# Adding the first slot of each chunk on VectorE instead of TensorE, in a product-key expert layer

## The reference

```
q = (xt @ w_query).reshape(t, 8, 2, 128)
sk = einsum('thcd,ckd->thck', q, sub_keys)          # two sets of 128 keys
top_s, top_i = top_k(sk, 16)                        # product keys: 16 x 16 candidates
idx, gate = the 16 best of the candidates, softmax of their scores      # per token, per head
h = einsum('thkd,td->thk', peer_u[idx], xt)
a = gate * gelu(h)
out = einsum('thk,thkd->td', a, peer_v[idx])        # 8 heads x 16 experts = 128 rows of 1024 per token
x = x + out
```

## Time and profile before

| what | value |
|---|---|
| median of 3 runs | 3075.08 us (3071.18 to 3080.69) |
| profiled execution, first to last instruction (span) | 3067.0 us |
| what the metric has around the span | 8.1 us (3075.08 - 3067.0); the profiled execution has no other time than its span |
| PE, DVE busy | 2694.1 us (88%), 2135.5 us (70%) |
| ACT, POOL busy | 1193.2 us (39%), 1260.2 us (41%) |
| DMA | 1170.33 MB, mean 382 GB/s |
| chain that ended last | PE 43%, DMA 22%, DVE 20%, ACT 8%, issue 5%, POOL 2% |

### The profile page before, as it was taken

One profiled execution on the slowest core, in us unless ns is written; L12 is line 12 of the kernel. 1 busy time (PEld: TensorE's weight loads), 2 busy tenths in 40 slices (PEclk: granted clock), 3 DMA queues, 4 the chain that ended last, 5 costly groups with the idle time before them and its releaser, 6 DMA issues.

```text
span 3067.0 us, 29307 instructions
## 1 busy us (share of the span) xinstructions
PE 2694.1 (88%) x8608; PEld 1481.6 (48%) x8608; DVE 2135.5 (70%) x5243; ACT 1193.2 (39%) x3444; POOL 1260.2 (41%) x1028
## 2 busy tenths in 40 slices
PE   7869899989998999788998999888999877877777
PEld 6656465445654555345554555435555332333333
DVE  4555577976657778866656778876756777776765
ACT  3322445753324545533223545653323323232232
POOL 0023343344334454444444444334444555445443
PEclk9789999999999999899999999989999999889989
DMA  4269999999999999999999999989999999999998
GB/s 160 67 255 414 368 397 394 378 354 401 398 420 415 407 419 417 361 358 404 413 415 420 397 378 421 393 331 368 412 420 421 420 418 422 405 420 417 418 416 353
DMA packets 173808, 1170.33 MB, mean 382 GB/s; under 512 B 19280, under 2 KB 19408, under 8 KB 42576
## 3 DMA queue, kind: packets, MB, share of 16 engines
q0 software_dynamic: 147456, 1073.81, 86.0%
q1 hardware_dynamic: 26192, 94.65, 8.1%
HBM read 1166.28 MB, written 2.10 MB: 381 GB/s over the span
## 4 chain that ended last, share of the span: by engine, by line
PE 43%; DMA 22%; DVE 20%; ACT 8%; issue 5%; POOL 2%; SPq 0%; DVEq 0%; ACTq 0%
PE ysum L543 29%; DMA gather<-experts,idx 22%; DVE gather L1028 10%; PE bank L404 9%; DVE sd L811 3%; PE bank L505 3%; ACT diag L750 2%; POOL gather L362 2%; ACT amp L742 2%; ACT L592 1%; PE bank L451 1%; PE bank L419 1%; ACT gel L735 1%; DVE shared L838 1%; ACT sd L592 1%
## 5 line engine op out<-in xcount | busy, mean ns | idle before, releaser
L543 PE MATMUL ysum<-gather,diag 128*128 128x512 f32 x4096 | 1920.7, 624 | 300.1 <-ACT diag L750 298.6
L362 POOL DMA_INDIRECT gather<-experts,idx x1024 | 1260.0, 1230 | 1785.1 <-PE ysum L543 1519.9
L1028 DVE CUSTOM_DVE_ANT_0 gather<-gather,xc 128x1024 f32<-128x1024 f32 x1024 | 1222.8, 1224 | 545.3 <-DMA gather<-experts,idx 543.0
L543 PEld LDWEIGHTS ysum<-gather,diag 128*128 128x128 f32 x4096 | 802.5, 200 | 1320.2 <-issue 926.5
L735 ACT ACTIVATE gel<-hdot 128x4 f32<-128x4 f32 x255 | 52.4, 205 | 1519.2 <-DVE hdot L1028 1501.7
L404 PE MATMUL bank<-xnT,w 128*128 128x256 f32 x1984 | 457.2, 385 | 7.4 <-DVE xnT L800 7.4
L404 PEld LDWEIGHTS bank<-xnT,w 128*128 128x128 f32 x1984 | 376.6, 192 | 86.0 <-issue 29.9
L750 ACT ACTIVATE diag<-cc,amp 128x128 f32<-128x128 f32 x1020 | 326.8, 387 | 35.8 <-PE ysum L543 35.0
L742 ACT ACTIVATE amp<-gel,gate 128x1 f32<-128x1 f32 x1020 | 216.9, 283 | 8.3
L811 DVE RECIPROCAL sd<-sd 128x256 f32<-128x256 f32 x60 | 105.1, 1751 | 128.5 <-ACT sd L592 128.3
L735 ACT ACT_TABLE_LOAD x124 | 159.1, 1283 | 2.2
(11 more groups left out here) (116 smaller groups left out, 1495.2 us busy)
## 6 DMA issues: line engine op xcount, KB each, us to landing
w<-weights SPq DMA_DIRECT2D x168, 512.0 KB
gather<-experts,idx POOLq DMA_INDIRECT x1024
y_out<-x SPq DMA_DIRECT2D x4, 512.0 KB, 8.0
x<-x_in SPq DMA_DIRECT2D x2, 512.0 KB, 5.3
g2b<-g_rows SPq DMA_DIRECT2D x2, 512.0 KB
x<-x_in SPq DMA_DIRECT2D x1, 1024.0 KB, 12.0
cc<-consts_in SPq DMA_DIRECT2D x1, 603.5 KB, 6.6
late<-late_in SPq DMA_DIRECT2D x2, 256.0 KB, 9.9
```

Source lines behind the costliest of these rows:

```text
L362: pool.indirect_dma_start(gather[:, n % SLOTS, :], None, uv_d[m // 2], bass.IndirectOffsetOnAxis(ap=idx[:, g % 2, k:k + 1], axis=0)).then_ ...
L543: mm = nc.tensor.matmul(ysum[:, hf * 512:(hf + 1) * 512], diag[:, n % NDIAG, :], gather[:, n % SLOTS, DM + hf * 512:DM + (hf + 1) * 512], ...
L1028: e = V.tensor_tensor_reduce(out=gather[:, n % SLOTS, 0:DM], in0=gather[:, n % SLOTS, 0:DM], in1=xc[:, :], scale=1.0, scalar=0.0, op0=ALU. ...
```

## The change

Slot 0 of each chunk (`n % 4 == 0`) no longer goes to PE. DVE multiplies the second half of its row with `amp` and adds it to a new SBUF buffer `yacc` (`add_slot`); at the first chunk of a tile pass it writes instead of adding. It does so for chunk `cg - 1` behind the four dots of chunk `cg`. `s_yv` counts these, and POOL waits on it for a buffer whose last slot was such a slot; the other three slots wait on `s_yc` as before, whose counts are now three a chunk. ACT makes no diagonal for slot 0. `add_tile` adds both `ysum` and `yacc` to `x`. The DMA scratch area that the program reserves in SBUF is set to 4096 bytes a partition.

```diff
+        yacc = sb("yacc", DM)
+        s_yv = sem("s_yv")
+        def free(eng, n):
+            if n % CH == 0:
+                eng.wait_ge(s_yv, n // CH + 1)
+            else:
+                eng.wait_ge(s_yc, pe_slots(n) + 1)
+        def pe_slots(n):
+            return n // CH * (CH - 1) + n % CH - 1
...
                         if n >= SLOTS:
-                            pool.wait_ge(s_yc, n - SLOTS + 1)
+                            free(pool, n - SLOTS)
                         pool.indirect_dma_start(
...
         def chunk_pe(pe, c):
-            for j in range(CH):
+            for j in range(1, CH):
...
-                pe.wait_ge(s_dg, n + 1)
+                pe.wait_ge(s_dg, pe_slots(n) + 1)
                 for hf in range(2):
-                    mm = nc.tensor.matmul(ysum[:, hf * 512:(hf + 1) * 512], diag[:, n % NDIAG, :],
+                    mm = nc.tensor.matmul(ysum[:, hf * 512:(hf + 1) * 512], diag[:, pe_slots(n) % NDIAG, :],
                                           gather[:, n % SLOTS, DM + hf * 512:DM + (hf + 1) * 512],
-                                          start=k == 0, stop=k == HEADS * TOPK - 1)
+                                          start=k == 1, stop=k == HEADS * TOPK - 1)
...
         def diagonals(act, c):
...
-            for j in range(CH):
+            for j in range(1, CH):
...
             def add_tile(tg):
-                dve.wait_ge(s_yc, (tg + 1) * HEADS * TOPK)
+                dve.wait_ge(s_yc, (tg + 1) * (HEADS * TOPK // CH) * (CH - 1))
                 t = tg % (SEQ // P)
-                V.tensor_tensor(x[:, t, :], ysum[:, :], x[:, t, :], ALU.add).then_inc(s_x, 1)
+                chain(dve, V.tensor_tensor(x[:, t, :], ysum[:, :], x[:, t, :], ALU.add))
+                V.tensor_tensor(x[:, t, :], yacc[:, :], x[:, t, :], ALU.add).then_inc(s_x, 1)
+            def add_slot(cg):
+                n = cg * CH
+                dve.wait_ge(s_a, n + 1)
+                row = gather[:, n % SLOTS, DM:2 * DM]
+                scale = amp[:, cg % 2, 0:1]
+                if cg:
+                    dve.wait_ge(s_yv, cg)
+                if cg % per_tile == 0:
+                    V.tensor_scalar(yacc[:, :], row, scale, None, ALU.mult).then_inc(s_yv, 1)
+                else:
+                    V.scalar_tensor_tensor(yacc[:, :], row, scale, yacc[:, :], ALU.mult, ALU.add).then_inc(s_yv, 1)
...
+                if cg:
+                    add_slot(cg - 1)
                 if c % per_tile == 0 and cg:
+                    dve.wait_ge(s_yv, cg)
                     add_tile(cg // per_tile - 1)
...
             if m == NBLK - 1:
+                add_slot(NBLK * CHUNKS - 1)
+                dve.wait_ge(s_yv, NBLK * CHUNKS)
                 add_tile(m * TT + 1)
...
-    nc = bacc.Bacc("TRN2", target_bir_lowering=False, num_devices=1)
+    nc = bacc.Bacc("TRN2", target_bir_lowering=False, num_devices=1, dynamic_dma_scratch_size=4096)
```

More of the change, by code:

```diff
@@ L532, in chunk_pe @@
         def chunk_pe(pe, c):
-            for j in range(CH):
+            for j in range(1, CH):
                 n = c * CH + j
                 k = n % (HEADS * TOPK)
-                if k == 0 and n:
+                if k == 1 and n > 1:
                     pe.wait_ge(s_x, n // (HEADS * TOPK))
-                pe.wait_ge(s_dg, n + 1)
+                pe.wait_ge(s_dg, pe_slots(n) + 1)
                 for hf in range(2):
-                    mm = nc.tensor.matmul(ysum[:, hf * 512:(hf + 1) * 512], diag[:, n % NDIAG, :],
+                    mm = nc.tensor.matmul(ysum[:, hf * 512:(hf + 1) * 512], diag[:, pe_slots(n) % NDIAG, :],
                                           gather[:, n % SLOTS, DM + hf * 512:DM + (hf + 1) * 512],
-                                          start=k == 0, stop=k == HEADS * TOPK - 1)
+                                          start=k == 1, stop=k == HEADS * TOPK - 1)
                 mm.then_inc(s_yc, 1)
@@ L726, in last_diagonals @@
                                      scale=gate[:, c // 4 % 2, k:k + 1]).then_inc(s_a, 1)
-                act.wait_ge(s_a, n + 1)
-                act.wait_ge(s_yc, n - NDIAG + 1)
-                nc.scalar.activation(diag[:, n % NDIAG, :], ident, ACT.Copy, scale=amp[:, c % 2, j:j + 1]).then_inc(s_dg, 1)
+                if j:
+                    p = pe_slots(n)
+                    act.wait_ge(s_a, n + 1)
+                    act.wait_ge(s_yc, p - NDIAG + 1)
+                    nc.scalar.activation(diag[:, p % NDIAG, :], ident, ACT.Copy, scale=amp[:, c % 2, j:j + 1])\
+                        .then_inc(s_dg, 1)
         def diagonals(act, c):
@@ L743, in diagonals @@
                                      scale=gate[:, c // 4 % 2, k:k + 1]).then_inc(s_a, 1)
-            for j in range(CH):
+            for j in range(1, CH):
                 n = c * CH + j
+                p = pe_slots(n)
                 act.wait_ge(s_a, n + 1)
-                if n >= NDIAG:
-                    act.wait_ge(s_yc, n - NDIAG + 1)
-                nc.scalar.activation(diag[:, n % NDIAG, :], ident, ACT.Copy, scale=amp[:, c % 2, j:j + 1]).then_inc(s_dg, 1)
+                if p >= NDIAG:
+                    act.wait_ge(s_yc, p - NDIAG + 1)
+                nc.scalar.activation(diag[:, p % NDIAG, :], ident, ACT.Copy, scale=amp[:, c % 2, j:j + 1]).then_inc(s_dg, 1)
         def peer_act(act, m):
```

## The result

The changed kernel takes 3978.79 us (median of 4, 3974.83 to 3980.06) against 3074.67 us for the one before on the same chip: ratio 1.294, 95% interval 1.292 to 1.296. 4055 us was forecast (1.319), in a range of 3800 to 4290.

A forecast was written before the change was run, and what follows sets the result against it. DMA transfers were taken as the floor before; after, a queue emptying once a chunk. 253 periods of 14.41 us with start and end give 3889, plus 142 and 22: 4053 us span, 4061 with 8.1; 4055 us put, range 3800 to 4290.

The forecast's parts named there:

- Only one gather in flight at the release: When add_slot(c) frees buffer 4c, only gather 4c + 8 can be in flight, so the DMA queue empties once a chunk.
- PE was to be below 60% busy: Sign listed as showing the forecast right: PE's busy share, 88% before, falls below 60%.
- The cycle of 14.41 us: From one buffer release to the next: 0.28 + 11.55 + 1.15 + 1.28 + 0.15 us, against 11.1 us a chunk before.
- POOL held up by DVE, 0.15 us a chunk: POOL's issue takes 1.87 us when a dot starts just before it, 0.94 otherwise; 0.15 us a chunk taken, ends 0 and 0.93.
- The latency fit: Skill's fit for a gather, 2.0 us plus bytes over 436 GB/s: 4.4 us against 5.68, making the sum 330 us less.
- Weight loads and late DVE chunks, 164 us: 134 weight loads, 0.85 of them counted, 142 us; DVE's routing and mixer slices beyond the hidden 8.5 us, 22 us.
- The sum: 3889 us from the periods and the end, plus 142 and 22: 4053 us of span, 4061 with 8.1 us around it.
- The gain (2964 us): Faster rival: release early enough, queue never empties, DMA at its best rate throughout, 2964 us; chance 0.03.
- The smaller scratch: Rival: the smaller DMA scratch holds fewer gathers at once; if only one fitted, 6100 us; chance 0.03.
- The 8.1 us: Time around the profiled span, added to 4053 us to give 4061; said to be all that separates span and runs.
- the shorter gap: Rival, same mechanism: landings at 10.64 us, no POOL delay, period 13.35 us, about 3730 us; chance 0.13.
- the longer one: Rival, same mechanism: third dot at 12.08 us, full 0.93 us POOL delay, period 15.72 us, about 4410 us; chance 0.09.

The follow-up runs named there:

- the hold alone: Kernel before, plus only POOL waiting to reuse slot 4c's buffer until the four dots of chunk c + 1 are done: 3796.63 us, ratio 1.234.
- the kernel with small loads: Changed kernel with each of the 134 weight loads after the first 34 cut to an eighth of its bytes: 3889.04 us, ratio 1.267.
- Added work alone: Kernel before plus one DVE multiply-add behind each chunk's dots, on data no gather touches, and the 4096-byte scratch: 3106.41 us, ratio 1.011.
- Three in flight: Changed kernel with add_slot(c) placed ahead of the third dot of chunk c + 1, same work: 3302.41 us, ratio 1.077.

## Why the prediction was right

*Only one gather in flight at the release.* Right. POOL waits for the add in 246 chunks, the DMA share is near the forecast one (0.76 in the last block, "0.7 to 0.75" was said; 287 GB/s, 290 was said), the hold alone reproduces four fifths of the loss, one buffer more gives 61% of it back. One sign failed: PE was to be below 60% busy and is at 66%, since its matmuls took longer at the lower granted clock (last section), which costs nothing here.

*The cycle of 14.41 us.* 14.66 in the last block. Its terms there: 0.27 (0.28 said), third landing 11.97 (11.55 + 0.15 said), 1.15, 1.28. The period after an undisturbed POOL issue is 14.38 (44 of 60), where I had 14.26: 0.12 x 253 = 30 us more. The three landings come 5.90, 9.47 and 11.97 us after POOL's start on average in the last block, where the first gathers of the run gave 5.68, 9.06 and 11.55. Gather 565 was not the only other one of the kernel before that met an empty queue, as the prediction has it: from 2034 to 2036 us the DMA share is 0.00 too, ahead of gather 637, whose dot VectorE took late.

*POOL held up by DVE, 0.15 us a chunk.* Right as a mean: 39 of 253 first issues lasted 1.5 us or more, and their periods were longer by 1.05 us in the last block (16) and 0.71 us before it (23), 33 us in all against 38.

As the Trainium skill says (SBUF — State Buffer, "SBUF: two separate sides"), a GpSimd operation that reads SBUF and starts behind a VectorE operation with two SBUF inputs waits it out: the issue takes 1.91 us at 3719.06, behind a dot, and 0.94 at 3705.07, in the trace above. Issues behind `add_tile`'s second add (both inputs in SBUF) take 1.82 us, those behind its first add (one input in PSUM) 0.94 us, 7 of each.

The latency fit of the Trainium skill (DMA: Bandwidth & Descriptors, "Anatomy of one DMA — SWDGE (gpsimd) path") gives an estimate of 4.4 us for such a gather; here it is 5.9 us on average in the last block (5.21 us in the shortest of its periods), and the measurement decides.

*Weight loads and late DVE chunks, 164 us.* The term that was mis-sized. Undisturbed periods are 14.70 us in blocks 0 to 2 and 14.38 in block 3: 0.32 x 192 = 61 us for both causes. I had put 0.85 of the loads' bytes beside flowing gathers. By the kernel with small loads they cost some 15 us: the DMA rests about 3.6 us in each cycle (share 0.75 of 14.66 us).

*The sum.* Minus 103 for that, plus 30 for the landings, minus 5 for POOL, plus 5 since the first gather went out at 193.7 us instead of 188.9, minus 2.5 since the end is 9.9 us behind the last dot, not 12.4: 75 us less than 4053, 3978; the span is 3978.3. The 8.1 us that the prediction adds around the span is not what the metric has there: every execution on record is 1.8 us longer than its span (3980.06 against 3978.3 here), and the rest of the 8.1 was the difference between two executions. With 1.8 the sum of 4053 gives the 4055 that was put, by luck. The prediction's 11.1 us a chunk (2864 over 256) is 11.2; nothing hangs on it.

*Rivals.* The gain (2964 us) is excluded by the kernel with slot 0 in no sum: even without DVE's part it is 3050. The smaller scratch made no difference with nine gathers in flight (3070.12 us). Added work alone is 37 us. The undisturbed period of 14.38 us lies between the 13.35 of the shorter gap and the 15.72 of the longer one: from an empty queue the landings were not spaced evenly, and the full 0.93 us of a held-up issue fell in 39 periods alone.

## What to carry to other kernels

Where one queue of transfers sets the pace, ask of every consumer that is moved how long it holds its buffer, and count the transfers still in flight when it lets go; that count times the time of one transfer must at least cover the hand-over plus the latency of a transfer from an empty queue (here 2.7 + 5.7 us against 2.5 for the one gather in flight). Three in flight, 7.5 us, are short of it (11.04 us a chunk). And it is a least count: four, 10 us, would cover it, and the kernel with four (the add ahead of the 2nd dot) still took 10.56 us a chunk in the last block against 10.09. 1.28 us of work on an engine with 543 us to spare cost 904 us where it stood, and 37 us where no buffer waited for it. An engine at 88% that stands in the chain may be waited for only because all buffers are full: leave its work out in a test before moving it.

## What the hardware showed that I had not expected

PE did a quarter fewer of its largest matmuls and was busy for only 54 us less (2639.9 against 2694.1): one took 759 ns on average where it had 624:

```profile
L554 PE MATMUL ysum<-gather,diag 128*128 128x512 f32 x3072 | 1830.8, 759 | 1192.5 <-ACT diag L765 1131.1
```

In the windows of the cycle above its granted clock is 0.50, the 1.2 GHz level, when it starts at 3705 after 5.69 us without work, and its 12 matmuls take 8.18 us, where 16 at the full 2.4 GHz (granted clock 1.00 in those 7.1 us) took 7.13. Over the last block it had 0.73 of the clock against 0.92. POOL's waits for these matmuls are 20.4 us in all, none over 0.3, so it cost next to nothing.

After an empty queue the second gather lands 3.6 us behind the first, the third 2.5 us behind the second (means of the last block, 9.47 - 5.90 and 11.97 - 9.47), though POOL has issued them 1.25 us apart. So a dry queue costs about 1 us more than the first gather's latency. The gathers' packets of 8 KB or more also took longer on average than in the kernel before, 344 ns in both stages against 323 and 316: the same bytes kept the DMA engines busy for 71.0% of 3978.3 us, 2825 us, where it had been 86.0% of 3067.0, 2638 us.
